# The last projection of a decoder trunk: more of its k pairs as seven block products, and its first two column groups worked as a pair

## The chip, the cores and the metric

The kernel runs on one core of a Trainium2 chip. The metric is the device time of one execution in microseconds, as the median of several runs. Beside it stands a profiled execution, whose records give the start and the length of each instruction; all rows below are from that one.

## The reference: what is computed

The input x is a float32 array of 256 rows by 4096 columns. One decoder layer is applied to it: a norm, a projection of all columns, four attention branches, their merge and output projection, a residual addition, a second norm, and a channel mixer that picks experts. The change is in the last step of the mixer alone:

```
act = jax.nn.gelu(jnp.einsum('bsd,ed->bse', xn, u).astype(jnp.float32)).reshape(B * S, PEER_EXPERTS)
coef = gates * jnp.take_along_axis(act, experts, axis=-1)
wmat = jnp.zeros((B * S, PEER_EXPERTS), jnp.float32).at[jnp.arange(B * S)[:, None], experts].add(coef)
return (wmat.astype(v.dtype) @ v).reshape(B, S, -1)
```

So `wmat` is 256 by 4096, `v` is 4096 by 4096, and the result is added to the rows h that came out of the first half of the layer.

## The kernel before

Every large product is worked in chunks of weights. A chunk is 256 rows of the weight matrix (two k tiles of 128) by 512 columns, 512 KB in float32. Chunks are numbered through the whole program (`s`); a ring of four places (`RING`) holds them in three forms: `w_raw` as loaded, `w_hi` as ScalarE (ACT) rounds it for TensorE, and `w_lo`, the rest, which VectorE (DVE) subtracts. For each chunk TensorE (PE) waits for `w_hi`, issues hi·hi and lo·hi products (8 matmuls of 512 columns), waits for `w_lo`, and issues the 4 that take it: 12 matmuls, which end in `chunk_used`. ACT may make `w_hi` of chunk s once chunk s-4 is used up, so ACT and DVE run at most some three chunks ahead of PE. SyncE (SP) loads `w_raw` of chunk s once `w_lo` of chunk s-4 is made. Each engine has its instructions in one fixed order, written out in the program: in its turn for chunk s, ACT does `hi(s)` and then the side work that `between(s)` lists for this s, and DVE does `lo(s)`, then its own `between(s)`. A side task that waits holds up the `w_hi` or `w_lo` behind it.

The last product (called V) has eight column groups of 512, with 16 chunks each, 128 chunks from `CH_V` on. I write c for s - `CH_V`. Ahead of V lies the product U with its activation. While V begins, its left operand is still being finished: DVE multiplies `wmat` by the activations (`weigh_act`), ACT rounds it into `xt_hi` (`wmat_hi_part`), DVE makes `xt_lo` (`wmat_lo_part`), up to c = 14. The activations of the last group of U go through DRAM to be rearranged; ACT issues these transfers, and at c = 9 it waits in its own queue for the stores, before it loads them back (`act_t`).

Groups 0 and 1 are worked one after the other, in plain chunks. Groups 2 to 7 are three pairs of groups (`V_PAIRS`, each 16 k pairs by two groups). In a pair the chunks of its two groups alternate, and for the k pairs in `fast` the two chunks, seen as 2 by 2 blocks against the 2 by 2 blocks of the left operand, are multiplied in Strassen's way with seven block products of 3 matmuls instead of eight: 21 matmuls instead of 24 (`fast_products`). These need sums of left blocks (`s_raw`, split in `s_hi` on ACT and `s_lo` on DVE, made once for all pairs) and sums of weight blocks (`t_raw` in `t_sums`, `t_hi`, `t_lo`, made for each fast k pair). Four of the products gather in the PSUM tile `side`, which DVE adds to the rows afterwards (`add_pure`). `FAST` holds six k pairs, (0, 2, 4, 6, 8, 10). The sums of left blocks are made at c = 20 to 23, `s_hi` at c = 26, the two `s_lo` at c = 27 and 28.

In the very last chunk PE writes part of its result into `side` again (`last_products`), and so waits there for `add_pure` of the last pair.

Of the kernel before, what the change touches and what calls it, by code (L numbers as in the profile page):

```python
# [95 lines left out]
NF = len(FAST)  # L96
# [128 lines left out]
def build(nc, io):  # L225
# [327 lines left out]
    with nc.Block() as block:  # L553
# [3 lines left out]
        def _(sp):  # L557
# [77 lines left out]
            stream(last, CH_F)  # L635
# [14 lines left out]
        def _(pe):  # L650
# [385 lines left out]
            def fast_products(pair, kp):  # L1036
# [38 lines left out]
                if first and pair.order in (1, 3, 4):  # L1075
                    pe.wait_ge(pure_free, pair.order)
# [87 lines left out]
            for s in range(CH_V, CH_V + CPG):  # L1164
                c = s - CH_V
                if c == 0:
                    bank(GN_V % 2, GN_V // 2)
                pe.wait_ge(wmat_lo, c + 1)
                products(GN_V % 2, s, s % RING, xt, 2 * c, 512, c == 0, c == CPG - 1)
                between(s)  # L1170

            def group_one():

                bank((GN_V + 1) % 2, (GN_V + 1) // 2)
                for s in range(CH_V + CPG, CH_F):
                    c = s - CH_V - CPG
                    products((GN_V + 1) % 2, s, s % RING, xt, 2 * c, 512, c == 0, c == CPG - 1)

            group_one()
# [5 lines left out]
        def _(act):  # L1185
# [271 lines left out]
            def between(s):  # L1457
# [57 lines left out]
                if s >= CH_U + CPG and (s - CH_U) % CPG == LEAD:  # L1515
                    put_act((s - CH_U) // CPG - 1)
# [45 lines left out]
            for s in range(CH_V + CPG):  # L1562
# [5 lines left out]
                pair = out_pair(s)  # L1568
# [8 lines left out]
            for s in range(CH_V + CPG, CH_F):  # L1577
                hi(s, s % RING, 1024, s // RING)
                if s == CH_F - 6:
                    act.wait_ge(s_made, 3)  # L1580
                    for i in range(2):
                        nc.scalar.activation(s_hi[:, 2 * i:2 * i + 2].rearrange("p i q t -> p (i q t)"),
                                             s_raw[:, 2 * i:2 * i + 2].rearrange("p i q t -> p (i q t)"),
                                             ACT.Copy).then_inc(s_hi_done, 1)
            for pair in V_PAIRS:
# [11 lines left out]
        def _(dve):  # L1597
# [649 lines left out]
            def t_sums(pair, kp):  # L2247
# [9 lines left out]
                if kp == pair.fast[0] and pair.order in (1, 3, 4):  # L2257
                    dve.wait_ge(pure_free, pair.order)
# [92 lines left out]
            for s in range(CH_V + 2 * CPG):  # L2351
# [6 lines left out]
                pair = out_pair(s)  # L2358
# [12 lines left out]
                if pair:  # L2371
                    pair_tasks(pair, kp, i, OUT_PAIRS[1] if pair.order == 0 else None)
                between(s)

            for pair in V_PAIRS:
                before = V_PAIRS[pair.order - 3] if pair.order > 2 else None
                after = V_PAIRS[pair.order - 1] if pair.order < 4 else None
                for kp in range(CPG):
# [8 lines left out]
                    if kp == 1:  # L2387
                        if before:
                            end_of_pair(before, 1)
                        else:  # L2390
                            add_rows(1, CH_V, (GN_V + 1) % 2, h_rows)
# [21 lines left out]
        def _(pool):  # L2413
# [56 lines left out]
            for n in range(GRP - 2):  # L2470
                if n < 2:
                    pool.wait_ge(bank_free[(GN_V + n) % 2], (GN_V + n) // 2 + 1)
                else:
                    pool.wait_ge(block_free, 2 * (n - 1))
# [90 lines left out]
```

## Time and profile before

| what | value |
|---|---|
| median of 3 runs | 1912.88 us (1912.43 to 1913.54) |
| the profiled execution, whole time | 1913.45 us |
| its span, first to last instruction | 1911.4 us |
| PE busy | 1906.5 us, 100% of the span |
| DVE busy, ACT busy | 1423.9 us (74%), 976.7 us (51%) |
| granted TensorE clock | 1.00 of full speed |
| DMA | 412.72 MB, mean 216 GB/s |

The profiled execution took 1913.45 us, 2.1 us more than its span and 0.57 us more than the median of the runs. The busy share of PE counts a matmul from its start to its modelled end, and these overlap; its rate is read from the starts.

### The profile page before, as it was taken

What the parts mean: (1) busy time and instruction counts of PE and PEld (TensorE: products, weight loads), DVE (VectorE), ACT (ScalarE), POOL (GpSimd) and SP (SyncE); (2) the same over time, 40 slices, a digit from 0 to 9 for tenths busy, and PEclk for the clock granted to TensorE, in tenths of its full rate; (3) what the DMA queues carried; (4) which work ended last, traced back from release to release, by engine and by line L of the source; (5) the groups of instructions that cost most, each with busy time, mean ns of one, the idle gap of its engine ahead of it and who ended that gap; (6) DMA issues with size and microseconds to landing.
All of it is one profiled execution on the core that took longest, in us unless ns stands there. A gap on an engine that the chain in (4) does not pass through costs nothing.

```text
span 1911.4 us, 26402 instructions
## 1 busy us (share of the span) xinstructions
PE 1906.5 (100%) x9212; PEld 1573.0 (82%) x9212; DVE 1423.9 (74%) x2073; ACT 976.7 (51%) x1204; POOL 36.3 (2%) x49
## 2 busy tenths in 40 slices
PE   9999999999999999999999999999999999999999
PEld 8888888888888888888888888888887788888887
DVE  6578775575556889989765555788879877789896
ACT  6653644445566555546444464444444454555453
POOL 0010010000000000000000000000000000000000
PEclk9999999999999999999999999999999999999999
DMA  9976666655655669877787776677776668666664
GB/s 320 356 219 167 170 177 195 175 155 164 184 178 175 187 189 289 275 230 240 254 260 227 216 226 224 224 218 214 216 212 193 184 204 305 208 214 215 204 220 154
DMA packets 198834, 412.72 MB, mean 216 GB/s; under 512 B 45792, under 2 KB 124256, under 8 KB 198080
## 3 DMA queue, kind: packets, MB, share of 16 engines
q1 hardware_dynamic: 174048, 369.35, 63.0%
q10 hardware_dynamic: 20976, 25.19, 3.9%
q0 software_dynamic: 3696, 16.65, 2.4%
q8 instruction: 73, 1.20, 0.3%
q14 instruction: 41, 0.34, 0.1%
HBM read 390.15 MB, written 20.97 MB: 215 GB/s over the span
## 4 chain that ended last, share of the span: by engine, by line
PE 99%; DMA 0%; SPq 0%; ACT 0%; DVE 0%; issue 0%
PE acc L659 26%; PE acc L662 26%; PE acc L666 26%; PE acc L707 3%; PE acc L709 3%; PE acc L713 3%; PE acc L1132 1%; PE side L1022 1%; PE side L1023 1%; PE side L1024 1%; PE side L837 1%; PE acc L1138 1%; PE acc L1063 1%; PE acc L1069 1%; PE acc L1064 1%; PE side L948 1%
## 5 line engine op out<-in xcount | busy, mean ns | idle before, releaser
L1602 DVE TENSOR_TENSOR w_lo<-w_raw,w_hi 128x1024 fp32r<-128x1024 f32 (+1 forms) x654 | 792.3, 1214 | 436.3 <-ACT w_hi L1195 433.1
L1195 ACT ACTIVATE w_hi<-w_raw 128x1024 fp32r<-128x1024 f32 (+1 forms) x654 | 686.4, 1052 | 719.1 <-PE acc L666 597.5
L659 PE MATMUL acc<-w_hi,xt_hi 128*128 128x512 f32 x1396 | 378.5, 393 | 0.0
L662 PE MATMUL acc<-w_hi,xt_lo 128*128 128x512 f32 x1396 | 373.5, 389 | 0.0
L666 PE MATMUL acc<-w_lo,xt_hi 128*128 128x512 f32 x1396 | 373.4, 389 | 0.0
L662 PEld LDWEIGHTS acc<-w_hi,xt_lo 128*128 128x128 f32 x1396 | 262.1, 188 | 55.1
L666 PEld LDWEIGHTS acc<-w_lo,xt_hi 128*128 128x128 f32 x1396 | 262.1, 188 | 54.8
L659 PEld LDWEIGHTS acc<-w_hi,xt_hi 128*128 128x128 f32 x1396 | 259.1, 188 | 53.4 <-issue 1.8
L659 PE MATMUL acc<-w_hi,x_hi 128*128 128x512 f32 x640 | 175.1, 395 | 0.0
L662 PE MATMUL acc<-w_hi,x_lo 128*128 128x512 f32 x640 | 171.8, 390 | 0.0
L666 PE MATMUL acc<-w_lo,x_hi 128*128 128x512 f32 x640 | 171.2, 389 | 0.0
L662 PEld LDWEIGHTS acc<-w_hi,x_lo 128*128 128x128 f32 x640 | 120.1, 188 | 25.7
L666 PEld LDWEIGHTS acc<-w_lo,x_hi 128*128 128x128 f32 x640 | 120.2, 188 | 25.3
L659 PEld LDWEIGHTS acc<-w_hi,x_hi 128*128 128x128 f32 x640 | 117.2, 188 | 22.4
L1337 ACT ACTIVATE gate<-acc 128x512 f32<-128x512 f32 x64 | 34.8, 596 | 36.8 <-PE acc L666 36.7
L1546 ACT ACTIVATE t_hi<-t_raw 128x1024 fp32r<-128x1024 f32 x36 | 36.1, 1051 | 15.7 <-PE acc L1024 15.7
L2275 DVE TENSOR_TENSOR t_lo<-t_raw,t_hi 128x1024 fp32r<-128x1024 f32 x36 | 42.4, 1218 | 0.8 <-ACT t_hi L1546 0.8
L659 PE MATMUL acc<-w_hi,zt_hi 128*128 128x512 f32 x128 | 34.5, 391 | 0.0
L666 PE MATMUL acc<-w_lo,zt_hi 128*128 128x512 f32 x128 | 34.2, 389 | 0.0
L662 PE MATMUL acc<-w_hi,zt_lo 128*128 128x512 f32 x128 | 34.2, 389 | 0.0
L1847 DVE TENSOR_TENSOR gate<-acc,gate 128x512 f32<-128x512 f32 x48 | 30.8, 682 | 0.0
L1279 ACT ACTIVATE probs<-probs,small 128x128 f32<-128x128 f32 (+2 forms) x44 | 18.3, 417 | 22.0 <-DVE small L1760 21.9
(378 smaller groups left out, 1985.5 us busy)
## 6 DMA issues: line engine op xcount, KB each, us to landing
w_raw<-in_stream SPq DMA_DIRECT2D x504, 512.0 KB, 4.2
w_raw<-in_w_in SPq DMA_DIRECT2D x16, 496.0 KB, 3.9
w_raw<-in_w_in SPq DMA_DIRECT2D x16, 480.0 KB, 4.2
w_raw<-in_w_in SPq DMA_DIRECT2D x16, 464.0 KB, 3.8
w_raw<-in_w_in SPq DMA_DIRECT2D x16, 448.0 KB, 3.7
w_raw<-in_w_in SPq DMA_DIRECT2D x16, 432.0 KB, 3.8
w_raw<-in_w_in SPq DMA_DIRECT2D x16, 416.0 KB, 4.1
w_raw<-in_w_in SPq DMA_DIRECT2D x16, 400.0 KB, 3.8
```

What stands on the lines that cost most here:

```text
L659: pe.matmul(o[h], lhs(k0 + j, h)[0], wh[j], start=first and j == 0, stop=False)
L662: pe.matmul(o[h], lhs(k0 + j, h)[1], wh[j], start=False, stop=False)
L666: mm = pe.matmul(o[h], lhs(k0 + j, h)[0], wl[j], start=False, stop=last and j == 1)
L707: pe.matmul(o, lhs(k0 + j, h)[0], wh[j], start=first and j == 0, stop=False)
L709: pe.matmul(o, lhs(k0 + j, h)[1], wh[j], start=False, stop=False)
L713: mm = pe.matmul(o, lhs(k0 + j, h)[0], wl[j], start=False, stop=last and j == 1)
L1195: nc.scalar.activation(w_hi[:, slot, 0:width], w_raw[:, slot, 0:width], ACT.Copy).then_inc(hi_ready, 1)
L1337: e = nc.scalar.activation(gate[:, n % 2, h, :], acc[:, 1, h, :], ACT.Sigmoid)
L1546: nc.scalar.activation(flat(hi_tile[:, d]), flat(raw[:, d]), ACT.Copy).then_inc(t_hi_done, 1)
L1602: nc.vector.tensor_tensor(w_lo[:, slot, 0:width], w_raw[:, slot, 0:width], w_hi[:, slot, 0:width].bitcast(F32), ALU.subtract).then_inc(lo_ ...
L1847: nc.vector.tensor_tensor(dst, acc[:, 0, h, :], gate[:, n % 2, h, :], ALU.mult)\
L2275: nc.vector.tensor_tensor(flat(lo_tile[:, d]), flat(raw[:, d]), flat(hi_tile[:, d]).bitcast(F32), ALU.subtract).then_inc(t_lo_done, 1)
```

## The change

Groups 0 and 1 become a pair too (order 2), with the fast k pairs 8 and 10. For its first four k pairs it takes four chunks of group 0, then four of group 1 (`HEAD`), and alternates from there. The last pair gets a seventh fast k pair, 12, so the tiles of left sums hold seven blocks (`NF` = 7). The sums of left blocks are made at c = 9 to 12, `s_hi` in ACT's turn c = 13, both `s_lo` in DVE's turn c = 14, and the weight sums of the first fast k pair in turn c = 15. The last pair adds its `side` products in turns of k pair 15 instead of 13 and 14. The core of the diff:

```diff
 FAST = (0, 2, 4, 6, 8, 10)
-NF = len(FAST)
+FAST_LAST = FAST + (12,)
+NF = len(FAST_LAST)
...
-V_PAIRS = tuple(Pair(2 + m, CH_F + 2 * CPG * m, FAST, 2 + (m + 1) * NF) for m in range(PAIRS - 1))
+V_PAIRS = (Pair(2, CH_V, FAST[4:], 8), Pair(3, CH_F, FAST, 10), Pair(4, CH_F + 2 * CPG, FAST, 16),
+           Pair(5, CH_F + 4 * CPG, FAST_LAST, 22))
+HEAD = {0: 2, 2: 4}
...
+    head = HEAD.get(pair.order, 0)
+    return pair.at + (head * i + kp if kp < head else 2 * kp + i)
...
+                if pair.order == 2:
+                    pe.wait_ge(wmat_lo, kp + 1)
-                if first and pair.order in (1, 3, 4):
+                if first and pair.order in (1, 3, 4, 5):
                     pe.wait_ge(pure_free, pair.order)
...
+                if s == CH_V + 13:
+                    s_hi_part()
...
+            def s_hi_part():
+
+                act.wait_ge(s_made, 3)
+                act.wait_ge(wmat_lo, NF)
+                for i in range(2):
+                    nc.scalar.activation(s_hi[:, 2 * i:2 * i + 2].rearrange("p i q t -> p (i q t)"),
+                                         s_raw[:, 2 * i:2 * i + 2].rearrange("p i q t -> p (i q t)"),
+                                         ACT.Copy).then_inc(s_hi_done, 1)
...
-                if CH_F - 12 <= s < CH_F - 8:
-                    s_sum(s - (CH_F - 12))
-                if CH_F - 5 <= s < CH_F - 3:
-                    s_lo_part(s - (CH_F - 5))
-                if s == CH_F - 1:
-                    t_sums(V_PAIRS[0], 0)
+                if CH_V + 9 <= s < CH_V + 13:
+                    s_sum(s - (CH_V + 9))
+                if s == CH_V + 14:
+                    s_lo_part(0)
+                    s_lo_part(1)
...
                 if i == 0:
-                    dve.wait_ge(wmat_lo, CPG)
-                    dve.wait_ge(wmat_hi, CPG)
+                    dve.wait_ge(wmat_ready, 2 * NF - 1)
...
-                if kp in (13, 14):
+                if kp in (13, 14) and pair.fast[-1] < 12:
                     add_pure(pair, 2 * (kp - 13) + i)
+                if kp == 15 and pair.fast[-1] == 12:
+                    add_pure(pair, 2 * i)
+                    add_pure(pair, 2 * i + 1)
```

On DVE, before the change, the fourth sum of left blocks (`s_raw`) in turn c = 23, the two `s_lo` with a chunk's `w_lo` between them, and the first weight sums (`t_raw`) at the end of group 1 stand like this:

```order
L2211 TENSOR_TENSOR s_raw<-wmat,s_raw 128x768
L1602 TENSOR_TENSOR w_lo<-w_raw,w_hi 128x1024 x4
L2221 TENSOR_TENSOR s_lo<-s_raw,s_hi 128x1536
L1602 TENSOR_TENSOR w_lo<-w_raw,w_hi 128x1024
L2221 TENSOR_TENSOR s_lo<-s_raw,s_hi 128x1536
L1602 TENSOR_TENSOR w_lo<-w_raw,w_hi 128x1024 x3
L2261 TENSOR_TENSOR t_raw<-w_raw 128x1024
L2265 TENSOR_TENSOR t_raw<-w_raw,t_raw 128x512
L2266 TENSOR_TENSOR t_raw<-w_raw,t_raw 128x512
L1602 TENSOR_TENSOR w_lo<-w_raw,w_hi 128x1024
L2281 TENSOR_TENSOR w_lo<-w_raw,w_hi 128x512
L2275 TENSOR_TENSOR t_lo<-t_raw,t_hi 128x1024 x2
```

With the change the same tasks stand in turns c = 12 to 17, from the fourth `s_raw` to the `w_lo` of chunk 17:

```order
L2206 TENSOR_TENSOR s_raw<-wmat,s_raw 128x896
L1602 TENSOR_TENSOR w_lo<-w_raw,w_hi 128x1024
L2108 TENSOR_TENSOR xt_lo<-wmat,xt_hi 128x512
L1602 TENSOR_TENSOR w_lo<-w_raw,w_hi 128x1024
L2108 TENSOR_TENSOR xt_lo<-wmat,xt_hi 128x512
L2216 TENSOR_TENSOR s_lo<-s_raw,s_hi 128x1792 x2
L1602 TENSOR_TENSOR w_lo<-w_raw,w_hi 128x1024
L2256 TENSOR_TENSOR t_raw<-w_raw 128x1024
L2260 TENSOR_TENSOR t_raw<-w_raw,t_raw 128x512
L2261 TENSOR_TENSOR t_raw<-w_raw,t_raw 128x512
L1602 TENSOR_TENSOR w_lo<-w_raw,w_hi 128x1024
L2276 TENSOR_TENSOR w_lo<-w_raw,w_hi 128x512
```

Between the last `s_raw` and the first `t_raw` there were eight `w_lo`; now there are three, the two `s_lo` lie back to back, and two `xt_lo` lie among them.

On ACT, before the change, from the rounding of `wmat` (`xt_hi`) in turn c = 11 to the first `t_hi`:

```order
L1454 ACTIVATE xt_hi<-wmat 128x512
L1195 ACTIVATE w_hi<-w_raw 128x1024
L1454 ACTIVATE xt_hi<-wmat 128x512
L1195 ACTIVATE w_hi<-w_raw 128x1024 x13
L1582 ACTIVATE s_hi<-s_raw 128x1536 x2
L1195 ACTIVATE w_hi<-w_raw 128x1024 x6
L1552 ACTIVATE w_hi<-w_raw 128x512
L1546 ACTIVATE t_hi<-t_raw 128x1024 x2
```

And the same piece with the change:

```order
L1451 ACTIVATE xt_hi<-wmat 128x512
L1192 ACTIVATE w_hi<-w_raw 128x1024
L1451 ACTIVATE xt_hi<-wmat 128x512
L1558 ACTIVATE s_hi<-s_raw 128x1792 x2
L1192 ACTIVATE w_hi<-w_raw 128x1024 x3
L1551 ACTIVATE w_hi<-w_raw 128x512
L1545 ACTIVATE t_hi<-t_raw 128x1024 x2
```

The two `s_hi` moved thirteen chunks up, to stand directly behind the last `xt_hi` and ahead of the `w_hi` of chunk 14.

## Rows read from the trace of the kernel before

**Rows 1.** The page: busy time, chain that ended last; span and mean granted clock.

```profile
PE 1906.5 (100%) x9212; PEld 1573.0 (82%) x9212; DVE 1423.9 (74%) x2073; ACT 976.7 (51%) x1204; POOL 36.3 (2%) x49
PE 99%; DMA 0%; SPq 0%; ACT 0%; DVE 0%; issue 0%
...
core 0: 1911.4 us, clock 1.000
```

**Rows 2.** Stretches, us: length; busy (count) of PE, PEld, DVE, ACT, POOL; clock.

```profile
1572.70:1659.72 87.02, 87.02 (x386) 72.05 (x385) 64.77 (x68) 44.55 (x48) 3.56 (x5) 1.00 0.79 260
1742.66:1825.60 82.94, 82.94 (x368) 68.67 (x367) 71.11 (x76) 42.57 (x44) 1.43 (x2) 1.00 0.67 216
```

**Rows 3.** Timeline of PE: a fast k pair begins, and what follows begins.

```profile
1669.79 0.39 PE L1063 MATMUL side<-w_hi,xt_hi 128*128 128x512 f32 x1
...
1674.55 1.07 PE L659 MATMUL acc<-w_hi,xt_hi 128*128 128x512 f32 x4
```

**Rows 4.** Timeline of ACT: start, length in us; in brackets idle before, releaser.

```profile
1572.81 1.06 ACT L1195 ACTIVATE w_hi<-w_raw 128x1024 fp32r<-128x1024 f32 x1 [1.14 <-PE acc L666]
...
1589.13 1.06 ACT L1195 ACTIVATE w_hi<-w_raw 128x1024 fp32r<-128x1024 f32 x1 [1.14 <-PE acc L666]
1593.08 1.21 ACTq L1401 DMA_DIRECT2D act_t<-act_blocks  x2
1594.33 0.63 ACT L1454 ACTIVATE xt_hi<-wmat 128x512 fp32r<-128x512 f32 x1 [4.14 <-issue]
1594.87 1.04 ACT L1195 ACTIVATE w_hi<-w_raw 128x1024 fp32r<-128x1024 f32 x1
...
1602.65 0.64 ACT L1454 ACTIVATE xt_hi<-wmat 128x512 fp32r<-128x512 f32 x1 [0.76 <-DVE wmat L2099]
```

**Rows 5.** Timeline of DVE, turns c = 10 to 12.

```profile
1595.95 1.23 DVE L1602 TENSOR_TENSOR w_lo<-w_raw,w_hi 128x1024 fp32r<-128x1024 f32 x1 [3.29 <-ACT w_hi L1195]
1597.09 0.68 DVE L2108 TENSOR_TENSOR xt_lo<-wmat,xt_hi 128x512 fp32r<-128x512 f32 x1
1597.69 1.22 DVE L1602 TENSOR_TENSOR w_lo<-w_raw,w_hi 128x1024 fp32r<-128x1024 f32 x1
1599.58 0.69 DVE L2099 TENSOR_TENSOR wmat<-wmat,act_t 128x512 f32<-128x512 f32 x1 [0.67 <-DMA act_t<-act_blocks]
...
1601.93 0.69 DVE L2099 TENSOR_TENSOR wmat<-wmat,act_t 128x512 f32<-128x512 f32 x1
```

**Rows 6.** Timeline of ACT and DVE where the left sums are made and split.

```profile
1626.80 0.95 DVE L2211 TENSOR_TENSOR s_raw<-wmat 128x768 f32<-128x768 f32 x1
...
1636.33 2.85 ACT L1582 ACTIVATE s_hi<-s_raw 128x1536 fp32r<-128x1536 f32 x2
1639.08 1.04 ACT L1195 ACTIVATE w_hi<-w_raw 128x1024 fp32r<-128x1024 f32 x1
...
1641.30 1.75 DVE L2221 TENSOR_TENSOR s_lo<-s_raw,s_hi 128x1536 fp32r<-128x1536 f32 x1
1642.97 1.22 DVE L1602 TENSOR_TENSOR w_lo<-w_raw,w_hi 128x1024 fp32r<-128x1024 f32 x1
```

**Rows 7.** Timeline of DVE around one fast k pair.

```profile
1692.68 1.22 DVE L2261 TENSOR_TENSOR t_raw<-w_raw 128x1024 f32<-128x1024 f32 x1
1693.94 0.69 DVE L2265 TENSOR_TENSOR t_raw<-w_raw,t_raw 128x512 f32<-128x512 f32 x1
...
1695.27 1.22 DVE L1602 TENSOR_TENSOR w_lo<-w_raw,w_hi 128x1024 fp32r<-128x1024 f32 x1
1697.01 2.35 DVE L2275 TENSOR_TENSOR t_lo<-t_raw,t_hi 128x1024 fp32r<-128x1024 f32 x2
```

**Rows 8.** Timeline of PE in the kernel's first microseconds, after a wait.

```profile
8.83 0.88 PE L678 MATMUL acc<-w_hi,xt_hi 128*128 128x336 f32 x4 [0.90 <-ACT w_hi L1195]
```

**Rows 9.** Timeline of DVE, first addition after the last pair.

```profile
1903.30 0.69 DVE L2399 TENSOR_TENSOR h_rows<-acc,h_rows 128x512 f32<-128x512 f32 x1 [3.13 <-PE acc L1138]
```

**Rows 10.** DMA issues, 1612 to 1640 us: KB each, median us to landing.

```profile
w_raw<-in_stream SPq DMA_DIRECT2D x10, 512.0 KB, 4.3
```

More of the change, by code:

```diff
@@ L108, with unrolled_pair @@
 OUT_PAIRS = (Pair(0, CH_OUT, FAST[4:], 0), Pair(1, CH_OUT + 2 * CPG, FAST, 2))
-V_PAIRS = tuple(Pair(2 + m, CH_F + 2 * CPG * m, FAST, 2 + (m + 1) * NF) for m in range(PAIRS - 1))
+V_PAIRS = (Pair(2, CH_V, FAST[4:], 8), Pair(3, CH_F, FAST, 10), Pair(4, CH_F + 2 * CPG, FAST, 16),
+           Pair(5, CH_F + 4 * CPG, FAST_LAST, 22))
 OUT_PLAIN = CH_OUT + 4 * CPG
+HEAD = {0: 2, 2: 4}
 def place(pair, kp, i):
-    return pair.at + (2 * i + kp if pair.order == 0 and kp < 2 else 2 * kp + i)
+    head = HEAD.get(pair.order, 0)
+    return pair.at + (head * i + kp if kp < head else 2 * kp + i)
 def placed(pair, s):
-    p = s - pair.at
-    return (p % 2, p // 2) if pair.order == 0 and p < 4 else (p // 2, p % 2)
-def out_pair(s):
+    p, head = s - pair.at, HEAD.get(pair.order, 0)
+    return (p % head, p // head) if p < 2 * head else (p // 2, p % 2)
+def unrolled_pair(s):
+    if CH_V <= s < CH_F:
+        return V_PAIRS[0]
     return OUT_PAIRS[(s - CH_OUT) // (2 * CPG)] if CH_OUT <= s < OUT_PLAIN else None
 def source(s):
-    pair = out_pair(s)
+    pair = unrolled_pair(s)
     if pair is None:
@@ L134, in source @@
     kp, i = placed(pair, s)
-    return CH_OUT + (2 * pair.order + i) * CPG + kp
+    return (CH_OUT + 2 * pair.order * CPG if pair in OUT_PAIRS else CH_V) + i * CPG + kp
 NCMP = (S - 32) // 16 + 1
@@ L475, in group_number @@
     def group_number(pair, i):
-        return GN_OUT + 2 * pair.order + i if pair in OUT_PAIRS else GN_V + 2 * (pair.order - 1) + i
+        return GN_OUT + 2 * pair.order + i if pair in OUT_PAIRS else GN_V + 2 * (pair.order - 2) + i
     def pair_bank(pair, i):
@@ L483, in s_tiles @@
     def s_tiles(pair, kp):
-        q = FAST.index(kp)
+        q = FAST_LAST.index(kp)
         if pair in V_PAIRS:
@@ L634, in _ @@
                     mix_load(MIX_LOAD[s])
-            stream(last, CH_F)
+            stream(last, CH_V)
+            for s in range(CH_V, CH_F):
+                load(io["stream"][source(s) - CH_MIX], s % RING, 1024, s - RING + 1)
             with sp.Fori(1, PAIRS) as m:
@@ L1115, in plain_products @@
                     pe.wait_ge(xt_lo_done, KT + kp + 1)
+                if pair.order == 2:
+                    pe.wait_ge(wmat_lo, kp + 1)
                 if kp == 0:
@@ L1162, in _ @@
                 between(s)
[L1164 to L1179, printed above, removed]
             for pair in V_PAIRS:
@@ L1514, in between @@
                         copy_queries(n)
-                if s >= CH_U + CPG and (s - CH_U) % CPG == LEAD:
+                if CH_U + CPG <= s < CH_V + CPG and (s - CH_U) % CPG == LEAD:
                     put_act((s - CH_U) // CPG - 1)
@@ L1561, in _ @@
             act.wait_ge(g_mix_loaded, 16)
-            for s in range(CH_V + CPG):
+            for s in range(CH_F):
                 if s < CPG:
@@ L1567, in _ @@
                             .then_inc(xt_hi_done, 1)
-                pair = out_pair(s)
+                pair = unrolled_pair(s)
                 kp, i = placed(pair, s) if pair else (None, None)
@@ L1575, in _ @@
                 between(s)
[L1577 to L1585, printed above, removed]
+            for pair in V_PAIRS[1:]:
                 for kp in range(CPG):
@@ L2256, in t_sums @@
                     dve.wait_ge(s_lo_done, 12)
-                if kp == pair.fast[0] and pair.order in (1, 3, 4):
+                if kp == pair.fast[0] and pair.order in (1, 3, 4, 5):
                     dve.wait_ge(pure_free, pair.order)
@@ L2288, in block_rows_of @@
                     return rows[:, h, n * 512:(n + 1) * 512]
-                n = 2 * (pair.order - 1) + i
+                n = 2 * (pair.order - 2) + i
                 return h_rows[:, h, n * 512:(n + 1) * 512]
@@ L2297, in add_pure @@
                     dve.wait_ge(t_used, pair.first_t + len(pair.fast))
+                    if pair.order == 2:
+                        dve.wait_ge(h_loaded, 64)
                     if pair in OUT_PAIRS:
@@ L2371, in _ @@
                 if pair:
-                    pair_tasks(pair, kp, i, OUT_PAIRS[1] if pair.order == 0 else None)
+                    pair_tasks(pair, kp, i, {0: OUT_PAIRS[1], 2: V_PAIRS[1]}.get(pair.order))
                 between(s)
-            for pair in V_PAIRS:
-                before = V_PAIRS[pair.order - 3] if pair.order > 2 else None
-                after = V_PAIRS[pair.order - 1] if pair.order < 4 else None
+            for pair in V_PAIRS[1:]:
+                before = V_PAIRS[pair.order - 3]
+                after = V_PAIRS[pair.order - 1] if pair.order < 5 else None
                 for kp in range(CPG):
                     s = place(pair, kp, 0)
-                    if kp == 1 and before:
+                    if kp == 1:
                         end_of_pair(before, 0)
@@ L2387, in _ @@
                     if kp == 1:
[L2388 to L2391, printed above, removed]
+                        end_of_pair(before, 1)
                     pair_tasks(pair, kp, 0, after)
@@ L2470, in _ @@
             for n in range(GRP - 2):
[L2471 to L2474, printed above, removed]
+                pool.wait_ge(block_free, 2 * (n + 1))
                 pool.dma_start(io["out"][:, :, n * 512:(n + 1) * 512],
```

7 lines of the change are left out of this document (2 added, 5 removed).

## The prediction

> **What bounds the kernel now.** I read the page first: by the chain that ended last, 99% of the span is PE, and nothing else has a share of one per cent [rows 1]. The busy share would not say this alone, since it counts overlapping matmuls. The stretches do. The 32 plain chunks of groups 0 and 1 hold 32 x 12 = 384 matmuls in 87.02 us, and a pair with six fast k pairs holds 384 - 6 x 3 = 366 in 82.94 us [rows 2]. Both give 0.2266 us from one matmul's start to the next. A fast k pair goes from 1669.79 to 1674.55, 4.76 us, which is 21 x 0.2267 [rows 3]. So in all of V each matmul starts when the one before lets it, at the full clock, and no wait of PE shows in any pair or at the change from one pair to the next. A matmul removed is worth 0.2266 us, and any work of DVE or ACT is free until it is late for a chunk. How late it may be has to be read from its own timeline.
>
> **What is removed.** The k pairs worked in Strassen's way go from 3 x 6 = 18 to 2 + 6 + 6 + 7 = 21. Three more save 3 x 3 = 9 matmuls: 9 x 0.2266 = 2.04 us. No load is saved, and the weights are the same 128 chunks.
>
> **What is added or moved, and is hidden.** DVE and ACT get three more sets of weight sums. Around a fast k pair DVE needs 2.59 us for the sums (1692.68 to 1695.27) and 2.35 us for `t_lo` [rows 7]. In a pair it has 71.11 us of work in 82.94 us [rows 2], and a seventh fast k pair in the last pair follows the rhythm of the six. The new change from pair 2 to pair 3 is of the kind that lies between the stretches now, which costs PE nothing [rows 2]; if the two blocks of PSUM weren't emptied ahead of PE, each would cost about an addition's 0.69 us [rows 9]. Group 1 now needs its bank at c = 4 instead of c = 16. ACT empties it in turn c = 3, whose `w_hi` starts at 1572.81 [rows 4]; PE comes to c = 4 some 10.8 us later. The last pair's `add_pure` moves to the end. I set the end of PE at T. The turn of the last chunk but one on DVE starts three to four chunks ahead, near T - 12.4; its `w_lo` and four additions take about 1.14 + 2.8, the last chunk's `w_lo` 1.14 and five additions about 3.4 (each 0.69 and a little for what waits on it). All is done near T - 3.9, while PE waits for it only half a chunk before its end, T - 1.4. The first addition behind, now after 3.13 us of idleness [rows 9], starts some 1.4 us later than now and has caught up before the last one. So I cost it at nothing; without those 2.5 us of cover it would go straight onto the end.
>
> **What is added and is not hidden.** The place is turns c = 9 to 17. There the left sums now stand among the end of `weigh_act` and `xt_lo`, just behind the stretch where ACT's own queue waits for the stores of the last activations: its `w_hi` of c = 9 starts at 1589.13, the transfers back at 1593.08, and the `w_hi` of c = 10 only at 1594.87 [rows 4]. Chunk c starts on PE at 1572.70 + 2.72c, since ACT's `w_hi` at c = 3 starts at 1572.81, released by PE [rows 4]. At c = 10 DVE's `w_lo` ends at 1597.18 [rows 5], and PE wants it at 1572.70 + 27.2 + 1.8 = 1601.7: 4.5 us of cover. From its start at 1595.95 on I lay DVE's queue out. Slots are from start to next start: `w_lo` 1.14 (1595.95 to 1597.09), a 512-column operation 0.60 (1597.09 to 1597.69) [rows 5]. The three left operations don't exist at 1792 or 896 columns. I scale them by 7/6, an estimate from the 768 and 1536 columns of now [rows 6]: `s_raw` 0.95 to 1.11, with 0.04 for the operation that waits on it (1692.68 + 1.22 to 1693.94 [rows 7]); both `s_hi` 2.75 to 3.21; one `s_lo` 1.67 to 1.95.
>
> - `s_raw` 1 at 1597.69, `w_lo` 11 at 1598.84, `wmat` at 1599.98 (now at 1599.58, when its transfer has landed [rows 5], so this wait goes), `xt_lo` 1600.58, `s_raw` 2 at 1601.18, `w_lo` 12 at 1602.33, `wmat` 1603.47, `xt_lo` 1604.07, `s_raw` 3 at 1604.67, ended 1605.78.
> - ACT stands in turn 13 and waits for it; everything behind waits too. `wmat` at 1601.93 lets `xt_hi` start at 1602.65, 0.03 after its end [rows 4, 5]. So `s_hi` starts at 1605.81 and `w_hi` 14 at 1609.02. PE needs that at 1572.70 + 14 x 2.72 = 1610.8, which still holds.
> - DVE takes `w_lo` 14 1.08 us after that start (as 1594.87 to 1595.95 [rows 4, 5]), at 1610.10, `xt_lo` 1611.24, both `s_lo` 1611.84, and `w_lo` 15 only at 1615.74, ended 1616.96. PE has started chunk 15 at 1613.49 and wants it after 8 matmuls, at 1615.30. With 0.05 us for the signal, PE waits 1.7 us.
> - Then the weight sums at 1616.88 and `w_lo` 16 at 1619.47, ended 1620.69. PE has ended chunk 15 at 1617.92 and wants it 6 matmuls later, at 1619.28: 1.5 us. The half `w_lo` 17 at 1620.61 costs 0.15 us more, and `t_lo` from 1621.21, whose first half ends at 1622.42, 0.9 us.
>
> The sum of the four waits is 4.2 us. It can be had in one step: without waits PE would want the first `t_lo` at 1572.70 + 16 x 2.72 + 9 x 0.2266 = 1618.25, and gets it at 1622.47. Behind this DVE catches up: the sums for k pair 10 start at 1625.76 and their `t_lo` ends near 1631.3, which PE wants at 1632.7. The load of c = 21, issued after 1621.3 and landing 4.3 us later [rows 10], comes just in time for these sums.
>
> Bounds of the wait: if the left operations took no longer than at 1536 columns, it is 4.2 - 3 x 0.16 - 0.46 - 0.56 = 2.7 us. From above: a load for k pair 10 that lands 6.8 instead of 4.3 us after its issue would find 1.3 us of cover there and add 1.2 us, 5.4 us in all. I take 4.2, since slots on DVE do scale (512 columns 0.60, 1024 1.14, 1536 1.67 [rows 5, 6]).
>
> The sum: 2.04 gained, 4.2 lost, net +2.2 us. On the profiled span of 1911.4 us this is 1913.6, and 1915.6 us for the whole execution against its 1913.45. The median of the runs is 1912.88, 0.57 us less than the profiled one, so I predict 1915.1 us. One measurement of this kernel can tell about 0.2%, 3.8 us, from no change; this would be 0.11%.
>
> **The rivals.**
>
> *DVE isn't late, the matmuls alone count.* For it: DVE has 4.5 us of cover at c = 10, and the same tasks later in V cost nothing. Against it: the queue above would have to be wrong by 4.2 us in 27. It gives 1912.88 - 2.04 = 1910.8 us. 14%.
>
> *The activation transfers land later.* One mechanism, at 1593.08, where ACT's queue waits [rows 4]. Now DVE behind it has its 4.5 us of cover; with the change it has none, and each us by which the stores land later goes into PE's wait at c = 15. Slower than 0.2% needs 3.8 + 2.04 = 5.9 us of wait, so it decides from 1.7 us later, with 2.5 us it gives 1917.6. For it: the DMA engines are busy for 79% even as a mean of the stretch [rows 2]. Against it: up to this point the program's transfers are the same. 10%.
>
> *The clock falls.* PE would stand still for 4.2 us in four pieces within 9 us. The nearest row is the 0.90 us of idleness ahead of 8.83 us, and the mean granted clock is 1.000 all the same [rows 1, 8]; no row shows a longer gap. At 1.2 instead of 2.4 GHz a matmul's 0.2266 us would be 0.45, so 3.4 us of half speed add 1.7 us and put the time over 1916.7. With 6 us of it: 1918 us. 3%. The Trainium skill, "TensorE: Matmul & The Clock Gate", in its part on the HAM clock gate, says that an engine left idle is put back to 1.2 GHz and has to be busy to return; by that rule the pieces here, with matmuls between them, could go either way. No row here shows a fall.
>
> *Faster by over 0.2%* would need 3.8 us, and 2.04 us are all that is removed: 2%.
>
> **How the numbers follow.** Forecast, a wait of 2.5 to 5.8 us: 71%. From it, and from the first rival, "within 0.2%" gets 85%; the two slower rivals give 13%, and 2% is left. The likeliest case's own range is 1913.4 to 1916.4. To hold 8 in 10 the range takes in the case without a wait, 1910.8, and part of the slower side: 1910.5 to 1917.0 us.
>
> **What would show it.** In the profile after: 9 fewer matmuls; PE, gapless until c = 15, with idleness of about 1.7 us there that ends with `w_lo`, and about 2.5 us more in the fast k pair behind it, released by `w_lo` and `t_lo`; ACT waiting some 2 to 3 us for `s_raw` ahead of `s_hi`; DVE without idleness from 1597 to 1623 us but for the wait on `w_hi` 14; a last pair shorter by 3 matmuls, 0.68 us, without a gap. The prediction is wrong if chunks 15 and 16 run gapless, if `w_lo` 15 ends before PE's eighth matmul of its chunk, or if the last pair shows a wait on `side`.

## The result, and the profile after

The changed kernel took 1916.69 us (median of 13 runs, 1915.28 to 1919.2), against 1913.05 us before (13 runs, 1912.31 to 1914.18): 3.64 us more, a ratio of 1.0019 with a 95% interval of 1.0011 to 1.0026. That is slower by 0.19%, at the edge of the 0.2% that I took for what can be told from no change. Forecast were 1915.1 us and +2.2 us.

The page after, its busy times, and the answer on span and mean granted clock, beside [rows 1]:

```profile
PE 1907.1 (100%) x9203; PEld 1572.0 (82%) x9203; DVE 1442.4 (75%) x2097; ACT 981.0 (51%) x1210; POOL 36.3 (2%) x49
...
core 0: 1914.8 us, clock 0.999
```

There are 9 matmuls less, as counted, and the span is 3.4 us longer. The profiled execution took 1916.72 us, next to the median. The waits of PE between 1588 and 1630 us, longest of their kind first (engine, line, what it waited for: us in total, times, longest):

```profile
PE acc L675 <- DVE w_lo L1602: 2.0, 1, 2.0
PE acc L668 <- ACT w_hi L1192: 1.0, 1, 1.0
PE side L1078 <- DVE w_lo L1602: 0.3, 1, 0.3
PE side L1031 <- DVE t_lo L2270: 0.3, 1, 0.3
```

Before the change PE had no wait there. These figures count from the modelled end of a matmul; what a wait costs is read from the starts. The timeline of PE (start, length, in brackets idle before and its releaser):

```profile
1608.18 1.07 PE L671 MATMUL acc<-w_hi,xt_lo 128*128 128x512 f32 x4
1609.08 1.07 PE L675 MATMUL acc<-w_lo,xt_hi 128*128 128x512 f32 x4
1611.14 1.17 PE L668 MATMUL acc<-w_hi,xt_hi 128*128 128x512 f32 x4 [0.99 <-ACT w_hi L1192]
...
1614.89 1.07 PE L671 MATMUL acc<-w_hi,xt_lo 128*128 128x512 f32 x4
1617.92 1.20 PE L675 MATMUL acc<-w_lo,xt_hi 128*128 128x512 f32 x4 [1.96 <-DVE w_lo L1602]
1618.95 0.39 PE L1072 MATMUL side<-w_hi,xt_hi 128*128 128x512 f32 x1
...
1621.64 0.79 PE L1078 MATMUL side<-w_lo,xt_hi 128*128 128x512 f32 x1 [0.34 <-DVE w_lo L1602]
1622.23 0.63 PE L1078 MATMUL acc<-w_lo,xt_hi 128*128 128x512 f32 x1
1622.66 0.47 PE L1078 MATMUL acc<-w_lo,s_hi 128*128 128x512 f32 x1
1623.47 0.47 PE L1031 MATMUL side<-t_hi,s_hi 128*128 128x512 f32 x1 [0.34 <-DVE t_lo L2270]
...
1626.30 1.07 PE L668 MATMUL acc<-w_hi,xt_hi 128*128 128x512 f32 x4
```

The first matmul of V starts at 1571.91 us here, 0.64 us earlier than in the profile before (1572.55), so without waits chunk c starts at 1571.91 + 2.72c. Chunk 14 starts at 1611.14 instead of 1610.0. The third part of chunk 15 starts at 1617.92, 3.03 us after the second, where four matmuls take 0.91. Behind each of these two waits the next group of four takes 0.1 us longer than usual. The fast k pair lasts from 1618.95 to 1626.30, 7.35 us where 21 matmuls take 4.76. In sum 1.2 + 2.2 + 2.6 = 6.0 us of delay, minus 2.04 us of matmuls, is +4.0 us from the start of V, and the 0.64 us by which V begins earlier leave the 3.4 us of the span. Everything behind runs without a gap: the last pair has 3 matmuls less and takes 82.23 us from its first start to its last, where it took 82.91: 0.68 us less.

ACT and DVE at the same place (timeline):

```profile
1588.49 1.06 ACT L1192 ACTIVATE w_hi<-w_raw 128x1024 fp32r<-128x1024 f32 x1 [1.14 <-PE acc L675]
1594.02 1.21 ACTq L1398 DMA_DIRECT2D act_t<-act_blocks  x2
1595.28 0.63 ACT L1451 ACTIVATE xt_hi<-wmat 128x512 fp32r<-128x512 f32 x1 [5.73 <-issue]
...
1606.77 3.29 ACT L1558 ACTIVATE s_hi<-s_raw 128x1792 fp32r<-128x1792 f32 x2 [0.97 <-DVE s_raw L2206]
1609.96 2.93 ACT L1192 ACTIVATE w_hi<-w_raw 128x1024 fp32r<-128x1024 f32 x3
```

```profile
1596.97 1.23 DVE L1602 TENSOR_TENSOR w_lo<-w_raw,w_hi 128x1024 fp32r<-128x1024 f32 x1 [3.95 <-ACT w_hi L1192]
...
1605.65 1.08 DVE L2206 TENSOR_TENSOR s_raw<-wmat,s_raw 128x896 f32<-128x896 f32 x1
...
1611.03 1.23 DVE L1602 TENSOR_TENSOR w_lo<-w_raw,w_hi 128x1024 fp32r<-128x1024 f32 x1 [2.56 <-ACT w_hi L1192]
1612.17 0.68 DVE L2108 TENSOR_TENSOR xt_lo<-wmat,xt_hi 128x512 fp32r<-128x512 f32 x1
1612.77 3.95 DVE L2216 TENSOR_TENSOR s_lo<-s_raw,s_hi 128x1792 fp32r<-128x1792 f32 x2
1616.64 1.22 DVE L1602 TENSOR_TENSOR w_lo<-w_raw,w_hi 128x1024 fp32r<-128x1024 f32 x1
```

The reader sees the queue of the prediction, link by link. From `w_lo` of c = 10 to `w_lo` of c = 15 it takes 1616.64 - 1596.97 = 19.7 us; I had 1615.74 - 1595.95 = 19.8. But it starts later: ACT waits 5.73 us for its stores, not 4.14 [rows 4], and brings `act_t` back 1.6 us later against the start of V (1594.02 - 1571.91 = 22.11, before 1593.08 - 1572.55 = 20.53).

### The profile page after: what moved, and what is told of

It reads as the page before. It is cut to its first block and busy times, and to the rows that moved or that the text cites. A ratio compares the mean times of both kernels' runs of the same rounds, so it can differ in the third digit from the quotient of the medians.

```text
span 1914.8 us, 26332 instructions
## 1 busy us (share of the span) xinstructions
PE 1907.1 (100%) x9203; PEld 1572.0 (82%) x9203; DVE 1442.4 (75%) x2097; ACT 981.0 (51%) x1210; POOL 36.3 (2%) x49
## 5 line engine op out<-in xcount | busy, mean ns | idle before, releaser
L668 PE MATMUL acc<-w_hi,xt_hi 128*128 128x512 f32 x1364 | 370.0, 393 | 1.0 <-ACT w_hi L1192 1.0
L675 PE MATMUL acc<-w_lo,xt_hi 128*128 128x512 f32 x1364 | 365.0, 389 | 2.0 <-DVE w_lo L1602 2.0
L671 PE MATMUL acc<-w_hi,xt_lo 128*128 128x512 f32 x1364 | 365.0, 389 | 0.0
L675 PEld LDWEIGHTS acc<-w_lo,xt_hi 128*128 128x128 f32 x1364 | 256.0, 188 | 56.0 <-DVE w_lo L1602 2.4
L671 PEld LDWEIGHTS acc<-w_hi,xt_lo 128*128 128x128 f32 x1364 | 256.0, 188 | 53.9
L668 PEld LDWEIGHTS acc<-w_hi,xt_hi 128*128 128x128 f32 x1364 | 253.1, 188 | 53.4 <-issue 3.2
L1545 ACT ACTIVATE t_hi<-t_raw 128x1024 fp32r<-128x1024 f32 x42 | 42.3, 1052 | 24.1 <-PE acc L1033 17.0
L2270 DVE TENSOR_TENSOR t_lo<-t_raw,t_hi 128x1024 fp32r<-128x1024 f32 x42 | 49.4, 1218 | 0.8 <-ACT t_hi L1545 0.8
L1276 ACT ACTIVATE probs<-probs,small 128x128 f32<-128x128 f32 (+2 forms) x44 | 18.3, 417 | 22.0 <-DVE small L1760 21.9
```

Of the source, the lines that this page charges most:

```text
L668: pe.matmul(o[h], lhs(k0 + j, h)[0], wh[j], start=first and j == 0, stop=False)
L671: pe.matmul(o[h], lhs(k0 + j, h)[1], wh[j], start=False, stop=False)
L675: mm = pe.matmul(o[h], lhs(k0 + j, h)[0], wl[j], start=False, stop=last and j == 1)
L1545: nc.scalar.activation(flat(hi_tile[:, d]), flat(raw[:, d]), ACT.Copy).then_inc(t_hi_done, 1)
L2270: nc.vector.tensor_tensor(flat(lo_tile[:, d]), flat(raw[:, d]), flat(hi_tile[:, d]).bitcast(F32), ALU.subtract).then_inc(t_lo_done, 1)
```

## The experiments

Every time below is a difference of medians to the kernel before, run on the same chip in the same session. "Delay" is the sum of what PE's starts in pair 2 (or group 0) are late beyond 0.2266 us each, read as above in one profile. One profile tells more than the medians: from the first matmul of V to the last, starts alone, it is 335.87 us before the change, 339.94 in the profile after (4.07 more), and in each experiment the figure given with it.

**e3_later: the left sums later, with later fast k pairs.**

```diff
-V_PAIRS = (Pair(2, CH_V, FAST[4:], 8), ...
+V_PAIRS = (Pair(2, CH_V, FAST_LAST[5:], 8), ...
-                if s == CH_V + 13:
+                if s == CH_V + 17:
                     s_hi_part()
-                if CH_V + 9 <= s < CH_V + 13:
-                    s_sum(s - (CH_V + 9))
-                if s == CH_V + 14:
-                    s_lo_part(0)
-                    s_lo_part(1)
+                if CH_V + 13 <= s < CH_V + 17:
+                    s_sum(s - (CH_V + 13))
+                if CH_V + 17 <= s < CH_V + 19:
+                    s_lo_part(s - (CH_V + 17))
```

> The kernel after, with the left sums moved down: pair 2 takes k pairs 10 and 12 as fast ones instead of 8 and 10, the four s_raw stand at c = 13 to 16, s_hi in ACT's turn 17, the s_lo in turns 17 and 18, and pair 2 adds its side products at k pairs 14 and 15. Nine matmuls are saved as in the kernel after. Theory A (the left sums stand too early, where DVE and ACT have no cover): DVE has over 7 us of cover at c = 17, so PE never waits in V, and the time is 2.04 us below before. Theory B (pairing groups 0 and 1 costs by itself, through more weight sums or the order of the loads): PE still waits some us in pair 2, and the time stays above before.

Measured: 1911.32 against 1913.3 us, -1.98 us (ratio 0.999, 0.9981 to 0.9999). In its profile V takes 334.12 us, 1.75 less than before: PE has no wait in pair 2; a quarter of a us is lost at the start of pair 3. Pairing groups 0 and 1 costs nothing by itself, and all 9 matmuls count. Theory B falls.

**e6_sums_only and e10_sums_only_again: the kernel before with the left sums alone at their new places.**

```diff
-                if CH_F - 12 <= s < CH_F - 8:
-                    s_sum(s - (CH_F - 12))
-                if CH_F - 5 <= s < CH_F - 3:
-                    s_lo_part(s - (CH_F - 5))
+                if CH_V + 9 <= s < CH_V + 13:
+                    s_sum(s - (CH_V + 9))
+                if s == CH_V + 14:
+                    s_lo_part(0)
+                    s_lo_part(1)
```

and `s_hi` from ACT's turn c = 26 to turn 13.

> The kernel before, with only the left sums moved up to the places that they have in the kernel after (s_raw at c = 9 to 12, s_hi in ACT's turn 13, both s_lo in DVE's turn 14, six blocks as before). Groups 0 and 1 stay plain, no matmul is saved. Theory A: w_lo of c = 15 is late as in the kernel after, less 1.5 us for the shorter operations, so PE waits 1.5 to 2.5 us once, and nothing behind it since no weight sums follow; time 1.5 to 2.5 us above before. Theory B: no wait, the time of before.

> Once more the kernel before with only the left sums moved up to c = 9 to 14, for a second profile. Theory A: PE waits for w_lo of c = 15 by about 0.1 to 0.5 us if ACT's wait in turn 9 is near 4 us, and one us more for each us that ACT waits longer. Theory B: no wait.

Measured: +0.83 us (1914.13 against 1913.3; ratio 1.0004, 0.9995 to 1.0013) and +0.23 us (1913.28 against 1913.25; 1.0001, 0.999 to 1.0011). The medians don't tell either from no change; the profiles do (V takes 336.40 and 337.19 us, 0.53 and 1.32 more than before). ACT's wait, and PE's only wait from 1588 to 1630 us (in all, times, longest), in the first and then in the second:

```profile
1594.18 0.63 ACT L1454 ACTIVATE xt_hi<-wmat 128x512 fp32r<-128x512 f32 x1 [4.04 <-issue]
PE acc L666 <- DVE w_lo L1603: 0.2, 1, 0.2
```

```profile
1594.68 0.63 ACT L1454 ACTIVATE xt_hi<-wmat 128x512 fp32r<-128x512 f32 x1 [4.88 <-issue]
PE acc L666 <- DVE w_lo L1603: 1.0, 1, 1.0
```

The wait is at the chunk that was named and is released by `w_lo`; the delay is 0.5 us with 4.0 us of ACT's wait, and 1.3 us with 4.9 us: 0.8 more for 0.8 more. That its size in the first was 0.5 and not 1.5 to 2.5 us came from my taking the 6.0 us of the profile after as the rule. So the left sums by themselves eat all of DVE's cover (the time by which its result is ready before PE wants it) and little more. In the kernel after, with seven blocks, 3.4 of the 6.0 us of delay lie at chunks 14 and 15, ahead of any use of weight sums; the other 2.6 us lie in the fast k pair, where the weight sums stand right behind sums that have left DVE no cover.

**e1_pair_only: without the seventh fast k pair.**

```diff
-FAST_LAST = FAST + (12,)
+FAST_LAST = FAST
```

> The kernel after without the seventh fast k pair of the last pair: six blocks of left sums again, 6 matmuls saved (1.36 us). Theory A: the left operations are a seventh shorter, so PE waits 4.5 us instead of 6.0 in pair 2; 3.1 us above before. Theory B: the whole wait of 6.0 us stays, 4.6 us above before.

Measured: +2.55 us (1915.85 against 1913.3; ratio 1.001, 1.0001 to 1.0019), nearer to theory A's 3.1 than to 4.6. The profile shows 3.8 us of delay (V takes 338.41 us, 2.54 more than before), and nearly half of it is of a kind that I hadn't put into the sum. ACT's wait, PE's two waits, and then the stretches (length, busy time and count by engine, then the granted clock, DMA share, GB/s):

```profile
1593.31 0.63 ACT L1451 ACTIVATE xt_hi<-wmat 128x512 fp32r<-128x512 f32 x1 [3.25 <-issue]
...
1618.32 0.50 PE L1078 MATMUL side<-w_lo,xt_hi 128*128 128x512 f32 x1 [0.85 <-DVE w_lo L1602]
...
1620.14 0.58 PE L1031 MATMUL side<-t_hi,s_hi 128*128 128x512 f32 x1 [0.73 <-DVE t_lo L2270]
```

```profile
1618.00:1620.10 2.10, 1.10 (x3) 0.48 (x3) 2.10 (x4) 2.10 (x3) 0.00 (x0) 1.00 0.40 76
1620.10:1623.80 3.70, 3.65 (x9) 2.91 (x10) 3.70 (x4) 1.66 (x3) 0.00 (x0) 0.54 0.70 260
1623.80:1627.00 3.20, 3.20 (x15) 2.61 (x15) 3.13 (x4) 2.08 (x3) 0.00 (x0) 1.00 0.82 273
```

Two waits, for `w_lo` and `t_lo`, delay PE by 1.1 and 1.0 us, and then the granted clock is 0.54 for 3.7 us: the matmuls of the fast k pair start 0.43 us apart instead of 0.23. That costs 1.7 us over nine of them. So the nearness to 3.1 is luck: the waits are 2.2 us, not 4.5, and the clock made up for most of that. Theory A's mechanism still holds, with the landing put in. DVE goes from `w_lo` of c = 10 to that of c = 15 in 18.3 us here, 1.3 less than with seven blocks, and ACT's wait is the shortest but one of the ten.

The 11 executions fall into two groups: the 5 with a mean granted clock of 1.000 took 1913.72 to 1914.76 us, the 6 with 0.999, the profiled one among them, 1915.85 to 1917.04. The medians of the two are 2.1 us apart.

**e2_seventh_only: only the seventh fast k pair, in the last pair.**

```diff
-V_PAIRS = tuple(Pair(2 + m, CH_F + 2 * CPG * m, FAST, 2 + (m + 1) * NF) for m in range(PAIRS - 1))
+V_PAIRS = (Pair(2, CH_F, FAST, 8), Pair(3, CH_F + 2 * CPG, FAST, 14), Pair(4, CH_F + 4 * CPG, FAST_LAST, 20))
```

and its side products added at k pair 15.

> The kernel before with only the seventh fast k pair in the last pair (and its side products added at k pair 15), groups 0 and 1 plain, left sums at their old places with seven blocks. Theory A: no wait anywhere, 3 matmuls less, 0.68 us below before. Rival (the late additions of the side products hold up the end): PE waits on them in the last chunk, no gain or some us of loss.

Measured: -0.98 us (1912.32 against 1913.3; ratio 0.9995, 0.9986 to 1.0004), which is too small to be told from no change, but in the profile V takes 335.19 us, 0.68 less than before, and PE's starts show no gap from 1560 us to the end. The late additions hold nothing up.

**e4_h_later: the loads of h away from the stores.**

```diff
-                pool.wait_ge(chunk_used, CH_V + 3 * q)
+                pool.wait_ge(chunk_used, CH_V + 10 + 3 * q)
```

> The kernel after with one edit: GpSimd's four loads of 1 MB each of the rows h, which start at c = 0, 3, 6 and 9, start at c = 10, 13, 16 and 19 instead, away from the stores of the last activations. Theory A with its cause of size (the landing of these stores on busy DMA engines sets where DVE's chain starts): ACT's wait in turn 9 falls from 5.7 us to under 4 us, DVE's chain starts 2 us or more earlier, and PE's waits fall from 6.0 us to 3 to 4 us: 1 to 2 us above before. Rival (DVE's and ACT's own work sets it, whenever the stores land): 3.6 us above before as in the kernel after.

Measured: +1.25 us (1914.3 against 1913.05; ratio 1.0007, 0.9998 to 1.0016); V takes 337.03 us in the profile, 1.16 more than before. ACT's wait for its stores is all but gone, and DVE's work at c = 9 to 14 then starts earlier; but one wait comes in its place:

```profile
1590.03 0.63 ACT L1451 ACTIVATE xt_hi<-wmat 128x512 fp32r<-128x512 f32 x1 [0.21 <-issue]
...
1625.31 1.23 DVE L2256 TENSOR_TENSOR t_raw<-w_raw 128x1024 f32<-128x1024 f32 x1 [2.23 <-DMA w_raw<-in_stream]
...
1631.01 0.47 PE L1031 MATMUL side<-t_hi,s_hi 128*128 128x512 f32 x1 [0.71 <-DVE t_lo L2270]
```

The delay at c = 15 is gone, that at c = 16 is 2.1 us, and 0.9 us are new at c = 20, where the weights of the second fast k pair now land among the loads of h and the weight sums wait 2.23 us for them. `w_lo` of c = 10 starts 21.15 us after the start of V here, 25.06 in the profile after, and the delay up to the end of c = 17 is 2.2 us instead of 6.0: 3.9 us earlier, 3.8 us less delay. So the landing of the stores does set where the chain starts, but with it removed the chain's own length still makes PE wait.

**e5_later_both: both edits.**

> Both edits at once: the left sums moved down as in the kernel with k pairs 10 and 12, and the loads of h moved down. If PE has no wait left in either, this is 2.04 us below before, no better than the former alone. If the later loads of h collide with the weights behind c = 10, PE waits there and the time is above that.

Measured: -1.57 us (1911.48 against 1913.05; ratio 0.9991, 0.9982 to 1.0), and V takes 334.12 us in the profile, as in e3_later. As good as that and no better. Where PE has its cover, the landing of the stores doesn't matter.

**e7_after_again: the changed kernel once more.**

> The kernel after once more, for a second profile of it. Theory A with the landing as its cause of size: ACT's wait in turn 9 and PE's wait move together, us for us, between executions. Rival (a fixed cost): PE waits 6.0 us in this profile too, whatever ACT's wait is.

Measured: +2.17 us (1915.22 of 8 runs against 1913.05; ratio 1.0011, 1.0001 to 1.0022); V takes 338.03 us in the profile, 2.16 more than before. ACT and PE in this profile:

```profile
1593.63 0.63 ACT L1451 ACTIVATE xt_hi<-wmat 128x512 fp32r<-128x512 f32 x1 [3.83 <-issue]
...
1616.27 1.20 PE L675 MATMUL acc<-w_lo,xt_hi 128*128 128x512 f32 x4 [1.33 <-DVE w_lo L1602]
...
1620.00 0.50 PE L1078 MATMUL side<-w_lo,xt_hi 128*128 128x512 f32 x1 [1.16 <-DVE w_lo L1602]
...
1621.83 0.47 PE L1031 MATMUL side<-t_hi,s_hi 128*128 128x512 f32 x1 [0.72 <-DVE t_lo L2270]
```

By its starts PE is delayed by 1.6, 1.4 and 1.1 us: 4.1 us (4.15 by finer figures), with 3.83 us of ACT's wait, against 6.0 us with 5.73. They move together, 1.9 us for 1.9 us.

**e8_early_sums: the same k pairs, the left sums in DVE's idle time.**

```diff
-                if s == CH_V + 13:
+                if s == CH_V + 11:
                     s_hi_part()
-                if CH_V + 9 <= s < CH_V + 13:
-                    s_sum(s - (CH_V + 9))
-                if s == CH_V + 14:
-                    s_lo_part(0)
-                    s_lo_part(1)
+                if s == CH_V + 9:
+                    for i in range(4):
+                        s_sum(i)
+                if CH_V + 13 <= s < CH_V + 15:
+                    dve.wait_ge(wmat_lo, 2 * NF)
+                    s_lo_part(s - (CH_V + 13))
```

> The kernel after with the same fast k pairs (8 and 10 in the first pair, seven in the last) and the same work, with only the places of the left sums changed: all four s_raw in DVE's turn c = 9, where it now stands idle while ACT waits for its stores, s_hi in ACT's turn 11, one s_lo in DVE's turn 13 and one in 14. Theory A (only the place of these sums makes the loss): w_lo of c = 15 ends near 1611.7 us, 3.6 us ahead of PE's want, and the first t_lo 1.1 us ahead; no wait of PE, 2.04 us below before. Rival (k pairs 8 and 10 are too early for the weight sums, whatever the left sums do): PE still waits 1 us or more at c = 16.

Measured: -2.06 us (1911.19 against 1913.25; ratio 0.999, 0.9981 to 0.9999). In the profile V takes 333.83 us, 2.04 less than before, and PE's starts show no gap in all of it. DVE in this profile:

```profile
1592.05 1.08 DVE L2207 TENSOR_TENSOR s_raw<-wmat 128x896 f32<-128x896 f32 x1
...
1596.43 1.22 DVE L1602 TENSOR_TENSOR w_lo<-w_raw,w_hi 128x1024 fp32r<-128x1024 f32 x1
...
1610.51 1.22 DVE L1602 TENSOR_TENSOR w_lo<-w_raw,w_hi 128x1024 fp32r<-128x1024 f32 x1
...
1615.97 2.35 DVE L2271 TENSOR_TENSOR t_lo<-t_raw,t_hi 128x1024 fp32r<-128x1024 f32 x2
```

The four sums lie between 1592.05 and 1596.43, where in the profile after DVE stood idle for 3.95 us. `w_lo` of c = 15 starts 6.1 us earlier than there. Not all of this is the place: the stores landed early in this profile (ACT waits 3.05 us), and against e7_after_again, with 3.83 us, it is 4.5 us. But all 11 executions of this kernel lie below the lowest of the kernel after, 1912.47 against 1914.52 us. The same work with the same k pairs, at other places, turns a loss into the full gain: the place of the left sums makes the loss, and the rival, that k pairs 8 and 10 come too early in any case, falls.

**e9_three_fast: a third fast k pair, 12, in the first pair.** The edits of e8_early_sums, and:

```diff
-V_PAIRS = (Pair(2, CH_V, FAST[4:], 8), Pair(3, CH_F, FAST, 10), Pair(4, CH_F + 2 * CPG, FAST, 16),
-           Pair(5, CH_F + 4 * CPG, FAST_LAST, 22))
+V_PAIRS = (Pair(2, CH_V, FAST_LAST[4:], 8), Pair(3, CH_F, FAST, 11), Pair(4, CH_F + 2 * CPG, FAST, 17),
+           Pair(5, CH_F + 4 * CPG, FAST_LAST, 23))
```

> The former kernel with a third fast k pair, 12, in the first pair, whose side products are then added at k pairs 14 and 15: 12 matmuls less than before. Theory A: no wait, 12 x 0.2266 = 2.72 us below before. If DVE's cover of 1 us at c = 16 is eaten up by one more set of weight sums, PE waits there and the gain falls back to 2 us or less.

Measured: -2.46 us (1910.79 against 1913.25; ratio 0.9987, 0.9978 to 0.9996), the fastest median of the study, ahead of both kernels. 2.72 us of matmuls, less 0.25 us of delay in the profile at the start of pair 3, are 2.47, and V takes 333.45 us there, 2.42 less than before. Against e8_early_sums it is 0.4 us, less than these runs can tell.

## Why the prediction was right

**The matmuls.** 9 x 0.2266 = 2.04 us. Right: V is 2.04 us shorter in the profile of e8_early_sums, where nothing waits, and 1.75 in that of e3_later, which loses 0.25 at the start of pair 3. The medians, 2.06 and 1.98 us less, agree more closely than their intervals (0.2 to 3.6 us) can tell.

**What was costed at nothing.** Right in each part: the change between pairs (the quarter of a us at the start of pair 3 shows only in the three kernels whose first pair has k pair 12 as a fast one), the bank of group 1, the seventh fast k pair (e2_seventh_only), and the end. The last additions of side products in the profile after, and the first addition behind them (beside [rows 9]):

```profile
1907.35 0.69 DVE L2313 TENSOR_TENSOR h_rows<-h_rows,sums 128x512 f32<-128x512 f32 x1
1908.08 0.69 DVE L2396 TENSOR_TENSOR h_rows<-acc,h_rows 128x512 f32<-128x512 f32 x1
```

PE ends near 1912.1, so they are done at T - 4.1, where I had T - 3.9.

**The chain of DVE and ACT.** Right in order and length. Put beside e7_after_again, whose stores landed about as they did before, the four waits were 1.7 + 1.5 + 0.15 + 0.9 = 4.2 us and are 1.6 + 1.4 + 1.1 = 4.1, the last two together. That the net forecast of +2.2 us is the +2.17 us of that session is closer than its interval, 0.2 to 4.2 us, can tell. The estimates for the longer operations (1.11, 3.21, 1.95 each) are 1.08, 3.19 (1606.77 to 1609.96) and 1.94 in the profile after. Two small things were left out, both upward. I took the end of a matmul, which releases ACT, for the start of the next, so that my start of V, 1572.70, is 0.15 us later than the first matmul's 1572.55; put right, the waits come to 4.35 us. And PE loses 0.1 us behind the last wait. In e7_after_again the chain then starts 0.24 us earlier against V than in the profile before and is 0.11 us shorter than I had it, which brings this back to 4.1.

**The signs named.** In the profile after PE was not gapless until c = 15. It waited for `w_hi` of chunk 14, where my queue had 0.5 us of room once the start of V is put right; the later start of the chain took that and made the chunk 1.2 us late; in e7_after_again chunk 14 is on time. ACT waits 0.97 us for `s_raw` ahead of `s_hi`, as my queue had it (about 1.0), not the 2 to 3 us that I wrote among the signs; only with the 1.88 us that it waits for `wmat` just before does it come near.

**What was mis-sized.** The term is the start of the chain, which I took from one profile as fixed. It depends on when ACT's stores land, and that differs from one execution to the next: ACT's wait there is 3.1 to 5.7 us in the ten profiles with the loads of h at their old places. Before, DVE's 4.5 us of cover hid this; now, in the profiles, each us is one of PE's. The first profile is 1.6 us late against the start of V, which accounts for the 6.0 us of delay in place of 4.2. This is what I had described as a rival with 10%, in the part of it that stays below its deciding point of 1.7 us. Whether the change itself makes the stores land later on average stays open; the repeated profile of the same kernel has 3.83 us, so it doesn't do so always.

**What else moved the time.** The first session had +3.64 us, the second +2.17, and the runs of the kernel after spread over 3.9 us, those of before over 1.9. The landing isn't shown to be all of that. In the first session 7 of the 13 executions of the kernel after have a mean granted clock of 0.999, the trace of a fall, and a median of 1917.11 us; the 6 with 1.000 have 1915.5, which is +2.45 us and nearly the forecast. In the second session all 8 have 1.000. The profiled execution shows the fall and hardly lost by it (below), e1_pair_only shows one that cost 1.7 us. Late stores make longer waits, and these may make the clock fall, so how much of the 1.6 us between the two groups is the one and how much the other stays open: only two executions with a fall have a profile.

**The rivals.** That DVE isn't late is refuted by the rows above. The clock did fall, and in 7 of 13 executions, where I gave 3% for a fall that decides. It cost what I had worked out (1.7 us) in e1_pair_only, and in the kernel after it didn't carry the median beyond 0.2%. The 3% was far too low for the event itself. In the profile after (length, busy times and counts, granted clock, DMA share, GB/s):

```profile
1618.00:1619.30 1.30, 1.30 (x6) 1.08 (x7) 1.27 (x2) 0.21 (x1) 0.00 (x0) 1.00 0.40 57
1619.30:1622.90 3.60, 3.26 (x9) 1.89 (x7) 3.57 (x5) 3.26 (x4) 0.00 (x0) 0.53 0.50 141
1622.90:1626.30 3.40, 3.06 (x14) 2.36 (x14) 3.40 (x4) 1.56 (x2) 0.00 (x0) 1.00 0.72 292
```

It cost almost nothing there, because PE would have waited for `w_lo` and `t_lo` in the same time. DVE's part of it:

```profile
1620.37 1.22 DVE L1602 TENSOR_TENSOR w_lo<-w_raw,w_hi 128x1024 fp32r<-128x1024 f32 x1
1621.51 0.68 DVE L2276 TENSOR_TENSOR w_lo<-w_raw,w_hi 128x512 fp32r<-128x512 f32 x1
1622.11 2.35 DVE L2270 TENSOR_TENSOR t_lo<-t_raw,t_hi 128x1024 fp32r<-128x1024 f32 x2
```

The three last products before `t_lo` start by 1622.66, and `t_lo`'s first half ends only near 1623.3. PE starts on it at 1623.47; by my estimate that is 0.1 us later than at the full clock, and the next start loses another 0.1.

## What to carry to other kernels

An engine that runs ahead of the bottleneck has a cover in us at each point of the program: how much earlier its result is ready than the bottleneck wants it. Before side work is moved, lay out its queue from the timeline, with what stands idle and what waits on a transfer, and put the work into the idle time (e8_early_sums) or where the cover is whole (e3_later). The same 9 matmuls went with +3.6 us (+2.2 in the second session) or -2.1 us, by the places of eight operations alone. Cover also hides the scatter of transfers: once it is used up, the scatter shows in the time, and one profile is no longer a fair basis for a sum. And once PE waits, look at the granted clock of every execution, not of the profiled one alone.

## What the runs showed of the hardware

TensorE's granted clock fell to about half (0.53 and 0.54 over 3.6 and 3.7 us, matmuls 0.43 us apart, the 1.2 GHz level) after short waits with matmuls between them: in the profile after behind delays of 1.2 and 2.2 us within 8 us, in e1_pair_only after delays of 1.1 and 1.0 us within 3 us. In e7_after_again delays of 1.6, 1.4 and 1.1 us left the mean granted clock at 1.000. By the mean clock of each execution (0.999 in both profiles with a fall, 1.000 in all the others; a fall much shorter than these would not show in three digits), it fell in 7 of 13 executions of the kernel after in the first session and in none of 8 in the second, in 6 of 11 of e1_pair_only and 4 of 11 of e4_h_later. It fell in none of the 74 executions of the six kernels whose profiles show at most one wait of PE in V, none of them with over 1.3 us of delay (e2_seventh_only, e3_later, e5_later_both, e6_sums_only and its repeat, e8_early_sums, e9_three_fast), nor in the 87 runs of the kernel before beside the experiments. So a wait can cost more than its own length, and whether it does differs from one execution to the next. The Trainium skill, "TensorE: Matmul & The Clock Gate", in its part on the HAM clock gate, describes the fall for an engine that was left idle; here it came without any single idle stretch longer than the 2.0 us of the waits above.
